# Second mixer's memory: an inner product moved ahead of the output shares, the router's offset product behind them

## The reference, cut to what matters

```python
o_a = attend_blocks(qa_l, ...)                      # 8 attention heads, 512 columns
h_l, _ = mlstm_bidir(*ml, ctx_states)               # the memory: 4 heads, both directions, 512 columns
y = jnp.concatenate([o_a, mlstm_out(h_l, ob_l)], axis=-1) @ w_out
...
x = x + m_lat[..., 2, :] * y
h = modulate_2(x, g_norm2[i], m_lat[..., 3, :], m_lat[..., 4, :])     # rmsnorm(x) * g * (1 + scale) + shift
x = x + m_lat[..., 5, :] * ec_moe(h, w_router[i], w_exp_gate[i], w_exp_up[i], w_exp_down[i])
```

## Time and profile before

| | us |
|---|---|
| three timed runs, median (lowest to highest) | 1753.82 (1752.71 to 1754.71) |
| the profiled execution's own time | 1751.88 |
| its span, first to last instruction | 1749.7 |
| PE busy / DVE busy / ACT busy in the span | 1525.9 / 691.9 / 379.8 |
| weights and data moved | 572.07 MB, mean 327 GB/s |

### The profile page before, as it was taken

The page is one execution under the profiler, slowest core; times in us unless marked ns, Lnnn a source line. Parts: engine busy times, 40 slices in busy tenths (PEclk is TensorE's granted clock), DMA queues, the critical chain, the costliest instruction groups (busy, mean ns, idle before and its releaser), DMA issues.

```text
span 1749.7 us, 21766 instructions
## 1 busy us (share of the span) xinstructions
PE 1525.9 (87%) x8898; PEld 983.3 (56%) x8898; DVE 691.9 (40%) x1556; ACT 379.8 (22%) x668; POOL 50.8 (3%) x70
## 2 busy tenths in 40 slices
PE   9999999999999999999987686868799886767776
PEld 6544878888888867676534242424354442434343
DVE  3378757568999666684111010100441100000002
ACT  2422520121210214233211111111132211111111
POOL 0000000001210000011000000000000000000000
PEclk9999999999999999999988888888999989898888
DMA  9625736756469905217999999999999999999996
GB/s 386 246 91 197 306 128 243 317 234 276 163 243 392 372 1 196 97 49 316 428 428 428 428 428 429 428 428 428 426 427 403 427 429 428 428 428 428 429 427 288
DMA packets 43900, 572.07 MB, mean 327 GB/s; under 512 B 7156, under 2 KB 7412, under 8 KB 8248
## 3 DMA queue, kind: packets, MB, share of 16 engines
q1 hardware_dynamic: 42832, 569.08, 78.0%
q10 hardware_dynamic: 1000, 2.05, 0.3%
HBM read 570.06 MB, written 1.05 MB: 326 GB/s over the span
## 4 chain that ended last, share of the span: by engine, by line
PE 61%; DMA 33%; DVE 3%; ACT 1%; issue 1%; SPq 1%; DVEq 0%; ACTq 0%
DMA ring<-in_w_exp_up_dram 31%; PE bank L520 17%; PE bank L1358 10%; PE bank L1039 9%; PE bank L1063 4%; PE bank L1388 2%; PE bank L528 2%; PE bank L1082 2%; PE bank L1438 2%; PE bank L1398 1%; PE bank L1345 1%; DMA ring<-in_w_exp_down_dram 1%; PE bank L685 1%; PE bank L742 1%; PE bank L695 1%
## 5 line engine op out<-in xcount | busy, mean ns | idle before, releaser
L1358 PE MATMUL bank<-ring,arena 128*32 128x512 f32 x1792 | 248.1, 705 | 185.8 <-DMA ring<-in_w_exp_up_dram 185.5
L1358 PEld LDWEIGHTS bank<-ring,arena 128*32 128x32 f32 x1792 | 69.1, 127 | 361.8 <-issue 360.6
L2840 DVE COPY arena<-bank 128x256 f32<-128x256 f32 x32 | 13.6, 425 | 557.3 <-PE bank L1374 557.3
L1039 PE MATMUL bank<-hT,ring 128*128 128x256 f32 x704 | 153.4, 379 | 0.0
L1039 PEld LDWEIGHTS bank<-hT,ring 128*128 128x128 f32 x704 | 133.3, 190 | 20.5 <-issue 2.6
L1388 PE MATMUL bank<-ring,arena 128*32 128x512 f32 x944 | 134.7, 710 | 3.3 <-DVE arena L2844 1.9
L2078 DVE SCALAR_TENSOR_TENSOR spare<-ring,spare 128x512 f32<-128x512 f32 x168 | 128.1, 763 | 5.0
L2003 ACT COPY arena<-bank 128x512 f32<-128x512 f32 x32 | 33.4, 1044 | 415.3 <-PE bank L1358 415.3
L1398 PE MATMUL bank<-arena 128*128 128x256 f32 x512 | 119.0, 385 | 1.8 <-DVE arena L2853 1.8
L1398 PEld LDWEIGHTS bank<-arena 128*128 128x128 f32 x512 | 94.6, 190 | 40.6 <-issue 29.0
L1345 PE MATMUL bank<-arena 128*128 128x32 f32 x960 | 110.7, 275 | 0.0
(11 more groups left out here) (390 smaller groups left out, 1632.9 us busy)
## 6 DMA issues: line engine op xcount, KB each, us to landing
ring<-in_packed_dram SPq DMA_DIRECT2D x64, 2048.0 KB, 12.3
ring<-in_w_exp_down_dram SPq DMA_DIRECT2D x58, 2048.0 KB, 17.3
ring<-in_w_exp_gate_dram SPq DMA_DIRECT2D x56, 2048.0 KB, 19.2
ring<-in_w_exp_up_dram SPq DMA_DIRECT2D x56, 2048.0 KB, 23.7
arena<-in_packed_dram SPq DMA_DIRECT2D x8, 2048.0 KB, 8.1
arena<-in_w_exp_up_dram SPq DMA_DIRECT2D x6, 2048.0 KB, 23.5
arena<-in_w_exp_gate_dram SPq DMA_DIRECT2D x6, 2048.0 KB, 24.8
ring<-in_packed_dram SPq DMA_DIRECT2D x5, 1024.0 KB, 12.6
```

The costliest lines, as they stand in the source:

```text
L1039: ins = pe.matmul(b[:, 0:T], x[:, k, j * 128:j * 128 + 128], hT[:, k, 0:T], start=(k == 0), stop=(k == KD - 1))
L1358: ins = pe.matmul(bank[0][32 * q:32 * q + 32, :], xe[:, k * CAP:(k + 1) * CAP], xs[q // 2][:, o:o + 512], start=(k == 0), stop=(k == KD - ...
```

## The change

It changes the order on three engines and nothing that is computed. On TensorE the shares 5 and 6 move ahead of the turn of block 0's weights, the turn of block 1's output and `inside(0)` ahead of the last share 7, and the router's two products behind share 7. ScalarE's list follows that order. On VectorE `from_inside(0)` moves ahead of `gated(1)`.

```diff
@@ TensorE
             inside(1)
             carried(0)
-            half_out(4)
+            for n in range(4, 7):
+                half_out(n)
+            turn_weights(0)
+            turn_out(1)
+            inside(0)
+            half_out(7)
+            G.over(("e_out", 0))
             router_shift(0)
             router_shift(1)
-            turn_weights(0)
-            half_out(5)
-            turn_out(1)
-            inside(0)
-            for n in range(6, 8):
-                half_out(n)
-            G.over(("e_out", 0))
             turn_out(0)
             shift_by_fours()
@@ ScalarE
             half_out(3)
             head_root(1)
-            half_out(4)
-            for layer in range(2):
-                evict(("sW", layer), shift_logits[layer], n=N_EXP)
+            for n in range(4, 7):
+                half_out(n)
             weights_turned(0)
             act.copy(fours.rearrange("p (k j i) -> p k j i", k=4, j=4),
...
-            half_out(5)
-            half_out(6)
             head_root(0)
             half_out(7)
+            for layer in range(2):
+                evict(("sW", layer), shift_logits[layer], n=N_EXP)
@@ VectorE
             head_normed(1)
             from_states(0)
+            from_inside(0)
             dve.wait_ge(sem("out_gates"), 1)
             gated(1)
-            from_inside(0)
             head_normed(0)
             gated(0)
```

## The result

The changed kernel takes 1756.15 us (median of 22 runs, 1753.61 to 1758.45), the kernel before 1752.83 us in the same sessions (22 runs, 1749.84 to 1756.03). The ratio is 1.0018, 95% interval 1.0012 to 1.0024: about 3.3 us slower. The profiled execution of the changed kernel took 1755.75 us, span 1753.8 us.

The account below looks back on a forecast made before the run. Expert-weight transfers run gapless from 829.28 us, so the chain ahead counts: -1.36 us order, +1.05 low clock, +1.7 second stretch give +1.4; +1.1 was taken on 1753.82, giving 1754.9 us, range 1751.5 to 1758.0.

Parts of the forecast that it names:

- One for one behind 829.28 us: First expert-weight issue after the pause: a microsecond gained or lost ahead of it comes out at the end one for one.
- Part 1: Shares 5 and 6 ahead of the turn of block 0's weights: the turn stays at 781.85 us, cost nothing.
- Parts 2 to 4: Memory's end: earlier inside(0), VectorE's new order, router products behind share 7; first output group 1.36 us earlier at full clock.
- Part 5: Low clock falls on gathered thin work before the first output groups; sum between -0.3 and +1.4 us, taken as +1.1.
- the bare order: Memory's end: had the clock not fallen before, the order itself is 0.45 us worse after the change.
- (a): Clock at the memory's end does not fall, or rises before the first output group: -1.4 to -0.3 us; chance 0.22.
- (c): Transfers, not TensorE, set 829.28 us, so the change does nothing at the end: exactly 0, 1753.8 us; chance 0.08.
- (d): Memory's end: new bank wait and low clock stay away, VectorE's 2.15 us come through: -2.2 us, 1751.6 us; chance 0.05.
- (b): Low clock holds through several output groups, about two and a half or more: price 3.5 to 5 us; chance 0.10.

Follow-up runs that it names:

- router_back: The changed kernel with the two router products and their copies back at their old place behind share 4; ratio to the kernel before 1.0039.
- the filled pair: The kernel before and the changed kernel, each with two more unread 128 x 256 products in both layers; ratios to the kernel before 0.9994 and 1.0006.
- router_only: The kernel before with only the two router products and their copies moved behind share 7; ratio to the kernel before 1.0033.
- spread_again: The changed kernel with VectorE's old order and wide shares placed anew between all thin work on TensorE; ratio to the kernel before 1.0002.
- wide_filler: The changed kernel with four unread products added, two between the router products and two behind the quartered product; ratio to the kernel before 1.0026.
- vector_order_back: The changed kernel with VectorE's old order, gated(1) ahead of from_inside(0); ratio to the kernel before 1.0005.
- thin_apart: The kernel before with the first router product and share 4 swapped, ScalarE's copy likewise; ratio to the kernel before 1.0002.
- spread: The changed kernel with wide shares between thin work, first try, leaving the first router product and two turns together; ratio to the kernel before 1.0016.
- before_filled: The kernel before with two more unread 128 x 256 products ahead of the turn of chosen tokens, in both layers; ratio to the kernel before 0.9994.

## Why the prediction was right, and where it was sized wrong

The measured 1756.15 us lie in the range, and the forecast's sign held; +3.3 us is just past the upper edge of the forecast's own range (+0.2 to +3.2), not at its +1.1.

*One for one behind 829.28 us:* right. In the fourteen profiles the first issue comes at 827.6 to 835.5 us. Behind it C1 is 486.9 to 487.2 us in ten, and 488.2 to 488.6 us in the four in which the clock fell at layer 1's first rows; D is 433.4 to 433.7 us but for one. What the kernels differ in before the first issue is not made up behind it.

*Part 1, cost nothing:* wrong by 0.4 us. I looked for cover on ScalarE and TensorE and left out GpSimd. Share 5 now ends earlier, so its addition on GpSimd meets VectorE's weighting of block 0. Timelines of GpSimd before and after:

```profile
779.12 0.72 POOL L2925 TENSOR_TENSOR xT<-xT,hT 128x256 f32<-128x256 f32 x1 [3.64 <-ACT hT L1921]
786.49 0.73 POOL L2925 TENSOR_TENSOR xT<-xT,hT 128x256 f32<-128x256 f32 x1 [6.66 <-ACT hT L1921]
```

```profile
780.77 0.78 POOL L2923 TENSOR_TENSOR xT<-xT,hT 128x256 f32<-128x256 f32 x1 [1.00 <-ACT hT L1920]
```

Before, GpSimd is idle from 779.84 to 786.49 us and the four instructions take 1.14 us; after, it adds from 780.77 us and they take 1.61 us. Block 1's, which met an addition at 770.22 us before too, took 1.61 us there. The Trainium skill, GPSIMD Engine Reference (section 1, Specifications), says that the engine shares its SBUF interfaces with VectorE and that VectorE's instructions with two SBUF inputs contend for them; these have two, and the trace agrees. `router_back` has VectorE's and the shares' changed order, but share 5's addition comes later, and the weighting takes 1.14 us again:

```profile
784.48 0.72 POOL L2925 TENSOR_TENSOR xT<-xT,hT 128x256 f32<-128x256 f32 x1 [4.58 <-ACT hT L1921]
```

```profile
780.49 1.14 DVE L2657 SCALAR_TENSOR_TENSOR arena<-arena 128x128 f32<-128x128 f32 x4
```

*Parts 2 to 4:* right in kind and order, each 0.3 to 0.6 us late, mostly by that 0.4 us: `inside(0)` 6.9 us after share 4 (6.6 forecast), output ready at 12.8 us (12.2), a pause of 0.47 us that ends with `gated(1)` (half a microsecond).

*Part 5, the low clock:* the step that was mis-sized. It fell as forecast and had, in the first profile, the two stretches forecast. But I let it begin behind the second router product; it began on it, 0.74 us more (2.59 for 1.85), and with VectorE's 0.4 us the first output group starts 0.3 and 0.6 us later than before in the first two profiles (16.58 us, as before, in the third), where I had it 0.6 us earlier. The output groups lose 1.5, 2.9 and 1.8 us (forecast 2.0). So against the first profile of before, A and B together measured +1.8, +3.5 and +1.8 us; the forecast's sum was +1.4 us, of which I took +1.1. That the number came out near is in part luck: I took the low clock before the change from one execution, and later profiles have 3.4 or 6.8 us of it before and 6.8 or 10.2 us after, so two executions can differ by 0.15 us (the filled pair) or by 3.5 us there. I also reckoned that the bare order, without any low clock, would cost 0.45 us; by the estimate at the end of the experiments it is about 0.1 us.

*What the forecast didn't have:* a fall at the first rows of a layer (C0 23.4 to 23.6 us for 22.1 to 22.4, C1 488.2 to 488.6 us for 486.9 to 487.2). It is not the change's alone: it is in the first profile of the changed kernel, in router_only and in spread_again, in layer 1 also in wide_filler, and absent in the other profiles of the changed kernel. Whether the change makes it more frequent stays open; with the filler the distance between the kernels went from 3.3 to 2.1 us, within the intervals.

*Rivals:* (a), no fall, and (c), no effect at the end, are excluded by the profiles, and (d), a gain, by the ratio; (b), the low clock through two and a half groups or more, is not reached: 16.70 - 13.80 = 2.9 us in the groups of the second profile, about 1.7 groups' worth. For (a) I wrote that the low stretches before were single, from the windows that I showed; the same trace has one at 0.50 from 838 to 842 us, right behind the stream's first issue. How the 3.3 us divide between the pause for the bank and the thin work is open in the runs: vector_order_back gives 2.3 us back, with an interval of about 1.9 us to either side, but only 0.6 us in its profile, which has the low clock still.

## What to carry to other kernels

When work on TensorE is re-ordered, look at what is wide and what is thin, not only at who waits for whom: the thin products moved behind the wide ones were held up by a single bank, for 0.47 us, and the longer low clock in and after them cost 1.7 us and more. What the thin products had done at their old place counts too: there they filled a wait for VectorE, which stood open for 3.19 us in router_only. Removing a fall at one place moved it to the next thin stretch in router_only and thin_apart, so place wide work between all of them, look at the granted clock of several executions, and reckon the time of the whole chain. And follow a moved product through every engine that reads it: the bank that it opens and the addition on GpSimd were both part of the price.

## What the runs showed of the hardware

The granted clock falls at other places and for other lengths in another execution of the same program: at the memory's end the low stretch was 3.4 us in two profiles of the old order and 6.8 us in the third, 6.8 us in two profiles of the changed one and 10.2 us in the third, and the runs of `spread` lie 6 us apart in two groups. An instruction of VectorE on two operands in SBUF took 0.82 us instead of 0.35 us when an addition of GpSimd ran beside it (the longest and the median of the eight at L2657 or L2655); four of them took 1.61 us beside the addition and 1.14 us without it (router_back). Added work made a kernel no slower where it filled a wait (before_filled, two products in each layer); where it ran at low clock it gained nothing (wide_filler, 1.0026).
